# First branch's gate input (two slabs): seven products of blocks in place of direct products

## What is computed

```python
proj = h @ w_in[l]
xa, ya, uv, zc, xbc, dtc, gates = jnp.split(proj, [...], axis=-1)
y_a = rglru_branch(xa, ya, ...) @ w_a_proj[l]     # scan(xa) * gelu(ya)
y_b = sgu_branch(uv, ...) @ w_b_proj[l]           # u * mixed(v)
y_c = ssd_branch(zc, xbc, dtc, ...) @ w_c_proj[l] # state space heads
...
    return h.astype(xa.dtype) * jax.nn.gelu(ya)
```

## Time and profile before

| | |
|---|---|
| median of 3 runs | 961.66 us (960.74 to 961.75) |
| profiled execution | 962.97 us, span 961.1 us |
| mean granted clock | 0.942 |
| PE busy | 826.0 us (86%) |
| DVE, ACT, POOL busy | 340.9, 191.8, 324.7 us |
| HBM read | 283.08 MB, 296 GB/s over the span |

### The profile page before, as it was taken

How to read it: one execution, slowest core, us unless ns; L and a number is a source line. 1 busy time by engine, 2 the same in 40 slices (tenths; PEclk the granted TensorE clock), 3 DMA queues, 4 the chain that set the end, 5 groups by cost and what they waited for, 6 DMA issues and landing times.

```text
span 961.1 us, 18480 instructions
## 1 busy us (share of the span) xinstructions
PE 826.0 (86%) x8065; PEld 650.2 (68%) x8065; DVE 340.9 (35%) x873; ACT 191.8 (20%) x357; POOL 324.7 (34%) x169
## 2 busy tenths in 40 slices
PE   9999999999999999999999996676676675585675
PEld 8999988889999999999887653333333332343332
DVE  3788323746264434244213451121121221221212
ACT  2342138731231000102012111111110111101102
POOL 5876630038998879996300000000000000000000
PEclk9999999999999999999999998888887988988988
DMA  9854534443564344556698999999999999999994
GB/s 313 254 176 177 177 131 157 151 141 123 176 218 159 133 159 166 176 176 228 223 430 336 401 429 432 430 428 436 426 432 434 425 436 428 428 436 430 424 430 195
DMA packets 58927, 284.95 MB, mean 296 GB/s; under 512 B 6308, under 2 KB 11256, under 8 KB 49912
## 3 DMA queue, kind: packets, MB, share of 16 engines
q1 hardware_dynamic: 54600, 280.84, 73.1%
q10 hardware_dynamic: 4272, 3.32, 1.2%
HBM read 283.08 MB, written 1.06 MB: 296 GB/s over the span
## 4 chain that ended last, share of the span: by engine, by line
PE 63%; DMA 31%; ACT 2%; DVE 2%; POOL 1%; issue 1%; SPq 0%; DVEq 0%; ACTq 0%; POOLq 0%
PE bank L1762 32%; DMA blk<-in_w_gate_up_dram 27%; PE bank L2037 9%; PE bank L1648 7%; PE bank L1757 5%; DMA ring<-in_w_down_dram 3%; PE bank L2002 2%; PE bank L1721 1%; PE bank L2066 1%; PE bank L2050 1%; PE bank L1918 1%; PE bank L1898 1%; DMA ring<-in_w_in_dram 1%; PE bank L1836 0%; PE bank L1857 0%
## 5 line engine op out<-in xcount | busy, mean ns | idle before, releaser
L1762 PE MATMUL bank<-blk,ring 128*128 128x128 f32 x1840 | 213.6, 275 | 0.4 <-POOL blk L592 0.4
L1762 PEld LDWEIGHTS bank<-blk,ring 128*128 128x128 f32 x1840 | 209.4, 192 | 2.0 <-issue 1.9
L2037 PE MATMUL bank<-blk,cbm 128*32 128x256 f32 x1024 | 77.9, 456 | 57.9 <-DMA blk<-in_w_gate_up_dram 57.9
L2037 PE MATMUL bank<-ring,cbm 128*32 128x256 f32 x992 | 75.7, 456 | 55.8 <-DMA ring<-in_w_gate_up_dram 55.8
L1488 DVE TENSOR_TENSOR cbm<-bank,gq 128x256 f32<-128x256 f32 x31 | 13.1, 424 | 264.4 <-PE bank L2002 264.4
L2037 PEld LDWEIGHTS bank<-blk,cbm 128*32 128x32 f32 x1024 | 35.0, 127 | 91.7 <-DMA blk<-in_w_gate_up_dram 64.1
L2037 PEld LDWEIGHTS bank<-ring,cbm 128*32 128x32 f32 x992 | 34.5, 127 | 88.3 <-DMA ring<-in_w_gate_up_dram 57.1
L1648 PE MATMUL bank<-blk,ring 128*128 128x256 f32 x384 | 85.4, 381 | 0.8 <-DVE blk L1410 0.8
L556 POOL TENSOR_TENSOR ring<-ring 128x1024 f32<-128x1024 f32 x20 | 47.4, 2371 | 97.0 <-DVE dec L1208 75.6
L1648 PEld LDWEIGHTS bank<-blk,ring 128*128 128x128 f32 x384 | 72.2, 190 | 11.6 <-DVE blk L1410 1.2
L1762 PE MATMUL bank<-ring 128*128 128x128 f32 x608 | 71.0, 275 | 0.0
(11 more groups left out here) (351 smaller groups left out, 1033.7 us busy)
## 6 DMA issues: line engine op xcount, KB each, us to landing
ring<-in_w_gate_up_dram SPq DMA_DIRECT2D x13, 4096.0 KB, 22.4
blk<-in_w_gate_up_dram SPq DMA_DIRECT2D x12, 4096.0 KB, 22.4
ring<-in_w_in_dram SPq DMA_DIRECT2D x19, 2048.0 KB, 7.8
ring<-in_w_down_dram SPq DMA_DIRECT2D x17, 2048.0 KB, 23.2
blk<-in_w_down_dram SPq DMA_DIRECT2D x13, 2048.0 KB, 24.1
blk<-in_w_gate_up_dram SPq DMA_DIRECT2D x8, 2048.0 KB, 20.0
ring<-in_w_gate_up_dram SPq DMA_DIRECT2D x5, 2048.0 KB, 13.4
ring<-in_w_kv_dram SPq DMA_DIRECT2D x4, 2048.0 KB, 8.0
```

Of the source, the lines that this page charges most:

```text
L1762: last = mm(out_[:, f], wt[:, k, f * P:(f + 1) * P], xt[:, k, :], start=k == 0, stop=k == 3)
L2037: last = mm(gu_bank(p)[c * WIN:(c + 1) * WIN, 0:2 * SEG], xe[:, xin, 4 * j + k, :], w[:, k, :, c, :], start=4 * j + k == 0, stop=4 * j + k ...
```

## The change

The two slabs of `ya` go through `strassen`, with the old heads placed inside: `heads(3)` and `heads(5)` behind the third of the seven products, `heads(4)` and `heads(6)` behind the sixth. S1 and S2 of `ya0`, `ya1` and `gA0` lie in the parameter tile `params` (whose first half is free once the `lg` matmuls are done), S4 and the middle results in half of a ring slot that holds the scan's factor before. ACT makes gelu over half of `ya` at a time, behind the fold. DVE's fold is cut in two, `fold_first` behind `weights(4)` and `weights(6)`, `fold_rest` behind the `exponents` of the same round. SP's first load of expert weights into `params` also waits for `gA0`.

```diff
@@ -82,8 +82,8 @@
         order += seven("v", h) + [f"lg{j}" for j in range(4 * h, 4 * h + 4)]
-    order += ["wst0", "u0", "u1", "y0", "u2", "y1", "u3", "y2", "ya0", "y3", "ya1", "y4", "ya2", "y5",
-              "ya3", "y6"]
+    order += ["wst0", "u0", "u1", "y0", "u2", "y1", "u3", "y2"]
+    order += ["y3", "y4"] + seven("ya", 0) + ["y5", "y6"] + seven("ya", 1)
     order += [f"sg{i}" for i in range(4)] + ["y7"]
@@ -214,17 +214,18 @@
         TA, TB = (block(b).rearrange("p (q k t) -> p q k t", q=4, t=P) for b in (6, 9))
-        GATE, EARLY = SEVEN["gA", 0], SEVEN["pA", 0]
+        GATE, EARLY, BRANCH = SEVEN["gA", 0], SEVEN["pA", 0], SEVEN["ya", 0]
...
-            two, one = (5, 8) if j < GATE else (10, 2) if j == GATE else (11, 14)
-            halves_ = [block(two)[:, 0:1024], block(two)[:, 1024:2048], block(one)[:, 0:1024]]
+            two = block(5) if j < BRANCH else params if j <= GATE else block(11)
+            one = block(8 if j < BRANCH else 10 if j < GATE else 2 if j == GATE else 14)
+            halves_ = [two[:, 0:1024], two[:, 1024:2048], one[:, 0:1024]]
             return [m.rearrange("p (k n) -> p k n", k=4) for m in halves_]
...
-            home = block(8 if j < GATE else 2 if j == GATE else 14)
+            home = block(8 if j < BRANCH else 10 if j < GATE else 2 if j == GATE else 14)
             return [home[:, 1024 + i * T:1024 + (i + 1) * T].rearrange("p (f t) -> p f t", f=2) for i in range(4)]
@@ -467,6 +468,7 @@
             sp.wait_ge(read["sg"], SGU_G)
+            sp.wait_ge(sem["unit_done"], U[last_of("gA", 0)] + 1)
             part(0, 0, TURNS[0])
@@ -549,9 +551,9 @@
                     pool.wait_ge(sem["unit_done"], U["y7"] + 1)
-                if j == GATE:
-                    pool.wait_ge(sem["w_ready"], KD - 1)
-                if j not in (0, GATE, EARLY):
+                if j == BRANCH:
+                    pool.wait_ge(sem["unit_done"], U[f"lg{KD - 1}"] + 1)
+                if j not in (0, BRANCH, EARLY):
                     pool.wait_ge(sem["product"], 6 * (j - 1) + 2)
@@ -575,7 +577,9 @@
                     pool.wait_ge(sem["yA_ready"], 1)
-                if j not in (0, GATE, EARLY):
+                if j == BRANCH:
+                    pool.wait_ge(sem["w_ready"], 3)
+                if j not in (0, BRANCH, GATE, EARLY):
                     pool.wait_ge(sem["product"], 6 * (j - 1) + 6)
@@ -606,7 +610,7 @@
             for name, h in (("xbc", 1), ("xbc", 2), ("xbc", 3), ("xa", 0), ("xa", 1), ("z", 0), ("z", 1), ("v", 0),
-                            ("v", 1)):
+                            ("v", 1), ("ya", 0), ("ya", 1)):
                 weights_1(name, h)
@@ -881,10 +885,20 @@
                 exps(i + 1)
-            for i in range(4):
-                evac(f"ya{i}", yaT, ACT.Gelu_apprx_tanh)
-                if i < 3:
-                    exps(5 + i)
+
+            def gelu_ya(h):
+
+                folded("ya", h)
+                m = yaT[:, 4 * h:4 * h + 4, :]
+                a.activation(m, m, ACT.Gelu_apprx_tanh).then_inc(sem["ya_ready"], 1)
+
+            mids("ya", 0)
+            exps(5)
+            exps(6)
+            gelu_ya(0)
+            mids("ya", 1)
+            exps(7)
+            gelu_ya(1)
@@ -1085,11 +1099,17 @@
             def fold(name, h, quarter):
+                fold_first(name, h, quarter)
+                fold_rest(name, h, quarter)
+
+            def fold_first(name, h, quarter):
+                sums(SEVEN[name, h], quarter(1, 1)).then_inc(read["s"], 1)
+
+            def fold_rest(name, h, quarter):
...
                 b2, b3 = bank(f"s{4 * j + 2}"), bank(f"s{4 * j + 3}")
-                sums(j, quarter(1, 1)).then_inc(read["s"], 1)
                 dve.wait_ge(sem["product"], 6 * j + 6)
@@ -1261,10 +1281,14 @@
                 weights(i)
+                if i in (4, 6):
+                    fold_first("ya", i // 2 - 2, columns(yaT, i // 2 - 2))
                 scan(1)
...
                     exponents(i + 2)
+                if i in (4, 6):
+                    fold_rest("ya", i // 2 - 2, columns(yaT, i // 2 - 2))
@@ -1281,7 +1305,7 @@
                                       ALU.mult, ALU.add))
-            dve.wait_ge(read["ya"], 4)
+            dve.wait_ge(sem["ya_ready"], 2)
             v.tensor_tensor(xaT, xaT, yaT, ALU.mult).then_inc(sem["yA_ready"], 1)
@@ -1738,7 +1762,7 @@
-            def strassen(name, h, x, t_, made, in_rows=False):
+            def strassen(name, h, x, t_, made, in_rows=False, third=None, sixth=None):
@@ -1769,12 +1793,16 @@
                 product(2, w21, t_[:, 1]).then_inc(sem["product"], 1)
+                if third is not None:
+                    heads(third)
                 pe.wait_ge(sem["weights_ready"], 4 * j + 3)
...
                 product(5, S4, x22).then_inc(sem["product"], 1)
+                if sixth is not None:
+                    heads(sixth)
                 pe.wait_ge(sem["combos_ready"], 4 * made + 4)
@@ -1829,7 +1857,7 @@
                 pe.wait_ge(sem["w_ready"], i + 1)
-                ps = begin(f"y{i}")
+                ps = bank(f"y{i}")
                 for h in range(2):
@@ -1842,12 +1870,12 @@
                 dense(f"u{i}", hT)
+                begin(f"y{i - 1}")
                 heads(i - 1)
-            for i in range(3):
-                dense(f"ya{i}", hT)
-                heads(3 + i)
-            dense("ya3", hT)
-            heads(6)
+            for h in range(2):
+                begin(f"y{2 * h + 3}")
+                begin(f"y{2 * h + 4}")
+                strassen("ya", h, hT, TA, 0, third=2 * h + 3, sixth=2 * h + 4)
             pe.wait_ge(sem["vn_ready"], 1)
@@ -1857,6 +1885,7 @@
                 end(last)
+            begin("y7")
             heads(7)
```

More of the change, by code:

```diff
@@ L347, in encoder_kernel @@
             conv_init silu_ready lam_ln alog_exp dt_ready dt_act dta_ready d_ready c_ready
-            ln_var ln_rms vn_ready z_ready v_ready pair_ready a2_ready a_ready a2_min mult_ready yA_ready
+            ln_var ln_rms vn_ready z_ready ya_ready v_ready pair_ready a2_ready a_ready a2_min mult_ready yA_ready
             cs_stored cs_taken exp_ready w_ready yz_ready csq_ready csum_ready
```

## The result

The changed kernel takes 965.58 us (median of 6 runs, 964.78 to 966.64), the kernel before in the same comparison 961.33 (6 runs, 960.17 to 961.75): ratio 1.0046, interval 1.0036 to 1.0056. It is **slower by 4.25 us**, and the interval leaves out 1. The forecast was 1.9 us slower; the time lies within the range, near its upper end. The profiled execution took 965.43 us, span 963.7.

A forecast was written before the change was run, and what follows sets the result against it. PE was taken to bound the changed stage, the experts' DMAs following one for one. A saving of 3.4 us and waits of 3.8 and 1.5 summed to +1.9, so 963.6 us, range 959.8 to 965.9.

The forecast's parts named there:

- What PE saves: In the two ya slabs, seven products of 1.79 us each replace four direct units: -3.4 us if PE never waits.
- Products slower than 1.8 us: Sign that the forecast is wrong: products in ya0 and ya1 above the 1.79 us each it counted on.
- The walk through ya: POOL's sums hold up DVE's exponents and weights, so PE waits 3.8 us before heads(4) and 1.5 before heads(6).
- The sum: Whole kernel: -3.4 + 3.8 + 1.5 = +1.9 us (+1.97 with the tenths kept), giving 963.6 us.
- the clock: Rival: PE's 3.8 us wait lets its granted clock fall, 1.7 us more, +3.7 in all, 965.3 us; chance 0.05.
- a clock under 1.00 before 570 us: Sign that the forecast is wrong: PE's granted clock falling anywhere before 570 us.
- The plan works: Rival: DVE's queue passes in one go when a sum ends, PE never waits: -3.4, 958.3 us; chance 0.14.
- The end does not follow: Rival: the experts' DMAs make up for the shift of PE's stage: 961.7 us; chance 0.02.

The follow-up runs named there:

- e6: The changed kernel with three of POOL's sums held until DVE has made the weights in question, same kernel as e1 run again: 958.78 us, ratio 0.9972 to the kernel before.
- e1: The changed kernel with three of POOL's sums held until DVE has made the weights in question: 958.68 us, ratio 0.9976 to the kernel before.
- e5: The changed kernel run once more as it is, in a later comparison: 965.07 us, ratio 1.004 to the kernel before.
- e3: The changed kernel with only the first middle sum (w21) of gA0 held on POOL until DVE's seventh weights: 963.82 us, ratio 1.0037 to the kernel before.

## Why the prediction was half right

- *"What PE saves", -3.4:* **mis-sized**, -2.62. I multiplied the product's 1.79 us by 14. In e6's timeline the products start at 179.91, 181.80, 183.59, and the next head at 185.47: 1.89, 1.79, 1.88. A product next to a head, before or behind it, takes about 0.09 more; nine of the fourteen are, and 0.8 us are gone. The rows I took them from have no heads between. "Products slower than 1.8 us" was a sign of being wrong, and it came.
- *"The walk through ya", waits of 3.8 and 1.5:* the mechanism and its places hold, e1 shows it by removing it. Measured 3.40 and 1.13. On the chain the stage starts at 180.04 and not 180.54, so the walk puts heads(4) near 195.3, and there they came; but the slower products made PE late by itself, so it waited less. No wait before heads(3) and heads(5), as forecast.
- *The sum:* -2.62 + 3.40 + 1.13 = +1.91, almost the forecast's +1.97. The two errors undo each other, since a slower product shortens the wait that follows. That is no merit of the sum.
- *The rival "the clock", 0.05:* **the step that failed.** I weighed a pause of 3.8 us against the DMA piece of 18.49 us only, and wrote "No fall in the rows for so short a wait". 18.49 us is a load from issue to landing; PE's idle time in front of the slow products was 6.40, the figure in brackets in the earlier trace rows. And the trace of before has 24 pauses of PE between 3.55 and 6.40 us among the experts, which I did not weigh. Timeline of PE before, two of the shortest:

```profile
651.18 2.89 PE L2037 MATMUL bank<-blk,cbm 128*32 128x256 f32 x32 [3.85 <-DMA blk<-in_w_gate_up_dram]
...
899.54 1.93 PE L2037 MATMUL bank<-ring,cbm 128*32 128x256 f32 x32 [3.55 <-DMA ring<-in_w_gate_up_dram]
```

The two pauses of 3.85 us had products of 2.78 and 2.89 us behind them instead of 1.93, those of 3.55 and 3.58 had 1.93. So there were rows with a fall behind a pause of 3.8 us, at a price of 0.9 to 1.0, and a chance of 0.05 was too low. In the stage the clock fell in both profiles of the changed kernel, and cost 2.87 and 1.60 where I had priced 1.7; a clock under 1.00 before 570 us was a sign of being wrong too. With it the sum is +4.8 and +3.5, and the medians say +4.25 and +3.76 (965.07 - 961.31). gA0 came at 220.98, not at about 218.7. The time lies in the range because the range took this rival in; my forecast by itself ended at 965.0. The Trainium skill (TensorE: Matmul & The Clock Gate, section HAM oscillation — how this bites in real kernels) describes PE throttled in a wait for data and starting cold behind it. The profiles of after and e5 agree; that of e3, with the same pause and clock 1.00, does not.
- *"The plan works", 0.14:* not so in the kernel as changed. But e1 and e6, where POOL's order leaves DVE alone, run it without a wait: 2.4 and 2.5 us faster than before.
- *"The end does not follow":* it follows. From gA0 to the end of the first long load the nine profiles agree within 0.9 us.

What stays open: why the same pause lets the clock fall in one execution and not in another, and why a product beside a head takes longer. Single times without a profile can't be split into the two falls of the clock, so how often each strikes is known by the estimate above at most. That e3's six times spread over 5.3 us fits a fall that comes and goes, but is not shown, and the spread is wider than the largest price seen, 2.87. A version with the heads in pairs, to have fewer products beside one, was not tried.

## What to carry to other kernels

Before work goes to an idle POOL, look at what DVE does in the same stretch out of SBUF: each sum lets one or two of DVE's instructions pass, and a short chain on DVE becomes as long as the row of sums. Here the sums did not have to move to another engine, only to wait: three held until DVE's chain was through turned 4 us of loss into 2.5 of gain. And a pause of PE is to be priced twice, as idle time and as the slow work that may stand behind it. Look for PE's own idle times of that length in the trace, not for a DMA piece of the chain, and give the fall a chance and not a yes or no: behind 3.3 us it came in two profiles here and stayed away in a third.

## What was not expected of the hardware

- After pauses of 3.3 us PE's clock fell to the lower level for a while in two profiles (granted 0.57 and 0.77 over the next 7.5 us, 2.87 and 1.60 us lost) and stayed at 1.00 in a third.
- It can fall with no idle time of PE on record before it: near 520 us, out of products of 36 columns and of 1, in four of nine profiles, of three changed kernels and of the one before. PE came 1.33 us later to the next long DMA piece each time, and the landing of that load came no later.
- Fourteen matmuls that nothing reads, in idle time, were worth 1.3 to 1.8 us.
